# Carrying the minus sign in the queries, so that the masking pass yields minus the row maximum

## The reference

```python
s = jnp.einsum('bqhgd,bjhd->bhgqj', q_c, k_c).astype(F32) * scale
if bias is not None:
    s = s + bias
s = jnp.where(valid, s, -jnp.inf)
if sinks is not None:
    m = jnp.maximum(jnp.max(s, axis=-1, keepdims=True), sk)
    p = jnp.exp(s - m)
    p = p / (jnp.sum(p, axis=-1, keepdims=True) + jnp.exp(sk - m))
else:
    p = jax.nn.softmax(s, axis=-1)
```

## Time and profile before

| | |
|---|---|
| median of 3 runs | 1069.41 us (1069.29 to 1070.34) |
| the profiled execution's own time | 1069.54 us |
| its span, first to last instruction | 1067.7 us |
| busy: PE, PEld, DVE, ACT, POOL | 1058.8, 928.8, 745.3, 627.2, 109.0 us |
| weights and tables read | 190.15 MB, 179 GB/s over the span |
| TensorE clock granted | full in all 40 slices |

### The profile page before, as it was taken

How to read it: one execution, slowest core, us unless ns; L and a number is a source line. 1 busy time by engine, 2 the same in 40 slices (tenths; PEclk the granted TensorE clock), 3 DMA queues, 4 the chain that set the end, 5 groups by cost and what they waited for, 6 DMA issues and landing times.

```text
span 1067.7 us, 16580 instructions
## 1 busy us (share of the span) xinstructions
PE 1058.8 (99%) x6592; PEld 928.8 (87%) x6592; DVE 745.3 (70%) x1130; ACT 627.2 (59%) x1066; POOL 109.0 (10%) x127
## 2 busy tenths in 40 slices
PE   8999999999999999999999999999999999999998
PEld 6988889888888898798888888889889989888887
DVE  6776585898855567768988555957655885766751
ACT  5754465776744567657766444547867644655630
POOL 4020000121100000001111000221000000111100
PEclk9999999999999999999999999999999999999999
DMA  7851356665664665367656656555433546665661
GB/s 267 299 178 60 119 176 224 212 196 173 204 197 162 234 202 173 96 194 244 195 176 208 193 167 226 156 198 178 119 118 119 178 151 202 199 193 170 215 192 39
DMA packets 56956, 192.27 MB, mean 180 GB/s; under 512 B 6832, under 2 KB 9776, under 8 KB 56880
## 3 DMA queue, kind: packets, MB, share of 16 engines
q1 hardware_dynamic: 56880, 191.22, 55.4%
HBM read 190.15 MB, written 1.05 MB: 179 GB/s over the span
## 4 chain that ended last, share of the span: by engine, by line
PE 93%; DVE 3%; POOL 1%; ACT 1%; issue 1%; DMA 0%; DVEq 0%; ACTq 0%; POOLq 0%
PE ps L982 28%; PE ps L1071 19%; PE ps L1063 15%; PE ps L1072 10%; PE ps L1359 5%; PE ps L1233 3%; PE ps L1133 2%; PE ps L1149 2%; PE ps L1170 1%; PE ps L1083 1%; DVE lo L1549 1%; PE ps L1218 1%; PE ps L1417 1%; POOL hr L571 1%; PE ps L1243 1%; ACT hi L626 1%
## 5 line engine op out<-in xcount | busy, mean ns | idle before, releaser
L1549 DVE TENSOR_TENSOR lo<-raw,hi 128x1024 fp32r<-128x1024 f32 (+2 forms) x347 | 430.4, 1262 | 88.1 <-ACT hi L626 85.5
L626 ACT ACTIVATE hi<-raw 128x1024 fp32r<-128x1024 f32 (+2 forms) x347 | 347.6, 1036 | 90.3 <-DMA raw<-in_weights 83.8
L1071 PE MATMUL ps<-y_both,hi 128*128 128x512 f32 x912 | 310.7, 389 | 0.0
L1072 PE MATMUL ps<-y_both,lo 128*128 128x256 f32 x912 | 251.8, 276 | 0.0
L1071 PEld LDWEIGHTS ps<-y_both,hi 128*128 128x128 f32 x912 | 171.2, 188 | 35.6
L1072 PEld LDWEIGHTS ps<-y_both,lo 128*128 128x128 f32 x912 | 171.2, 188 | 0.0
L1063 PE MATMUL ps<-y_both,hi 128*128 128x256 f32 x784 | 138.4, 280 | 0.8 <-DVE lo L1549 0.8
L1063 PEld LDWEIGHTS ps<-y_both,hi 128*128 128x128 f32 x784 | 119.0, 188 | 3.8 <-issue 2.6
L1063 PE MATMUL ps<-y_both,lo 128*128 128x256 f32 x392 | 108.8, 278 | 0.0
L982 PE MATMUL ps<-hi,y_both 128*128 128x512 f32 x352 | 94.1, 382 | 2.7 <-DVE lo L1549 1.4
L982 PE MATMUL ps<-hi,h_hi 128*128 128x512 f32 x294 | 91.0, 391 | 0.0
(11 more groups left out here) (289 smaller groups left out, 1467.5 us busy)
## 6 DMA issues: line engine op xcount, KB each, us to landing
raw<-in_weights SPq DMA_DIRECT2D x331, 512.0 KB, 4.3
gain<-in_gains SPq DMA_DIRECT2D x10, 512.0 KB, 7.7
raw<-in_weights SPq DMA_DIRECT2D x8, 384.0 KB, 7.0
bias<-in_rel SPq DMA_DIRECT2D x16, 128.0 KB, 2.4
raw<-in_weights SPq DMA_DIRECT2D x8, 256.0 KB, 2.5
mem_x<-in_mem SPq DMA_DIRECT2D x2, 512.0 KB, 9.9
h<-in_x SPq DMA_DIRECT2D x2, 256.0 KB, 2.8
h<-in_x SPq DMA_DIRECT2D x1, 512.0 KB, 5.9
```

What stands on the lines that cost most here:

```text
L626: act.activation(hi_at(n)[:, :w], raw_at(n)[:, :w], ACT.Copy).then_inc(hi_done, 1)
L1071: pe.matmul(dst, hi_at(n)[:, at], y_both[:, :, k, :], start=k == 0, stop=False)
L1072: mm = pe.matmul(dst[:, 0:S], lo_at(n)[:, at], y_hi[:, k, :], start=False, stop=k == KD - 1)
L1549: dve.tensor_tensor(lo_at(n)[:, :w], raw_at(n)[:, :w], hi_at(n)[:, :w].bitcast(F32), ALU.subtract).then_inc(lo_done, 1)
```

## The change

In stages a, m, f and x the scores come out negated, because the queries are copied with a negative constant (`scale=-HD ** -0.5`, and the selection matrix `c_pick`, which brings in fox's forget term, has -1 instead of 1). The masks of these stages hold +3e38 instead of -3e38 where a key isn't allowed (`least`). The masking pass takes the minimum, which is minus the row maximum, and writes it into `neg` itself; the negation L1682 and the wait before it are left for stage c alone. ACT's exponentials get a scale of -1 in these stages and wait for `row_max`. Stage a starts its minimum from the negated sink, which a new instruction makes once: `sinks_neg`, 128x8, behind `lb_d`. Stage c keeps its scores, its maximum and its negation.

```diff
-        pick[h, h], pick[64 + h, h] = 1, 1
+        pick[h, h], pick[64 + h, h] = -1, -1
...
-        "c_window": window.astype(f), "c_causal": causal.astype(f), "c_block": block_causal,
+        "c_window": least(window).astype(f), "c_causal": least(causal).astype(f), "c_block": block_causal,
...
+        def sign(stage):
+
+            return 1.0 if stage == "c" else -1.0
...
-                act.wait_ge(maxed, a + 1)
+                if stage == "c":
+                    act.wait_ge(maxed, hh + 1)
+                else:
+                    act.wait_ge(row_max, a + 1)
...
-                    e = act.activation(pr[:, a % 2, c], src, ACT.Exp, bias=neg[:, col, t:t + 1], accum_out=tot[:, col, t:t + 1])
+                    e = act.activation(pr[:, a % 2, c], src, ACT.Exp, scale=sign(stage), bias=neg[:, col, t:t + 1], accum_out=tot[:, col, t:t + 1])
...
-                act.activation(q_t[:, :, b * P:(b + 1) * P], split4(bank(b)), ACT.Copy, scale=HD ** -0.5).then_inc(a_evac, 1)
+                act.activation(q_t[:, :, b * P:(b + 1) * P], split4(bank(b)), ACT.Copy, scale=-HD ** -0.5).then_inc(a_evac, 1)
...
-                    dve.tensor_reduce(top[:, col, :], ps[:, a % 2, :].rearrange("p (t k) -> p t k", t=NT), AX.X, ALU.max).then_inc(row_max, 1)
+                    dve.tensor_reduce(neg[:, col, :], ps[:, a % 2, :].rearrange("p (t k) -> p t k", t=NT), AX.X, ALU.min).then_inc(row_max, 1)
...
-                        init = rows_in[:, hh:hh + 1] if stage == "a" else MASKED
-                        ins = dve.tensor_tensor_reduce(sc[:, a % 2, c], ps[:, a % 2, c], add, 1.0, init, ALU.add, ALU.max,
-                                                       top[:, col, t:t + 1])
+                        if stage == "c":
+                            ins = dve.tensor_tensor_reduce(sc[:, a % 2, c], ps[:, a % 2, c], add, 1.0, MASKED, ALU.add, ALU.max,
+                                                           top[:, col, t:t + 1])
+                        else:
+                            init = sinks_neg[:, hh:hh + 1] if stage == "a" else -MASKED
+                            ins = dve.tensor_tensor_reduce(sc[:, a % 2, c], ps[:, a % 2, c], add, 1.0, init, ALU.add, ALU.min,
+                                                           neg[:, col, t:t + 1])
                     ins.then_inc(row_max, 1)
-                dve.wait_ge(row_max, a + 1)
-                dve.tensor_scalar(neg[:, col, :], top[:, col, :], -1.0, None, ALU.mult).then_inc(maxed, 1)
+                if stage == "c":
+                    dve.wait_ge(row_max, a + 1)
+                    dve.tensor_scalar(neg[:, col, :], top[:, col, :], -1.0, None, ALU.mult).then_inc(maxed, 1)
...
             dve.tensor_tensor(lb_d[:, :], lb_in[:, 0:HB], lb_in[:, HB:2 * HB], ALU.subtract).then_inc(lb_sub, 1)
+            link(dve.tensor_scalar(sinks_neg[:, :], rows_in[:, :], -1.0, None, ALU.mult))
```

More of the change, by code:

```diff
@@ L144, in scores_mask, with least @@
         return np.concatenate([np.where(ok(q, k[:, :P]), 0, MASKED), np.where(ok(q + P, k), 0, MASKED)], 1)
+    def least(mask):
+        return np.where(mask < 0, -MASKED, 0)
     window = scores_mask(lambda a, b: (b // CHUNK <= a // CHUNK) & (b // CHUNK >= a // CHUNK - 2))
@@ L272, in build @@
         top = sb("top", [20, 2])
+        sinks_neg = sb("sinks_neg", [8])
         neg = sb("neg", [20, 2])
@@ L830, in _ @@
                     head_square(t, split4(bank(7)), 4, P)
-            act.wait_ge(maxed, 8)
+            act.wait_ge(row_max, 8)
             act.wait_ge(dve_sink, 1)
@@ L910, in heads_copy @@
                     act.activation(token_half(dst, kh, t), split4(bank(base + b)), ACT.Copy,
-                                   scale=HD ** -0.5 if kh == 0 else 1.0).then_inc(heads_evac, 1)
+                                   scale=-HD ** -0.5 if kh == 0 else 1.0).then_inc(heads_evac, 1)
             def branch_hi(i):
@@ L929, in _ @@
                         act.wait_ge(heads_turned, 8 + t + 1)
-                        act.activation(qc_t[:, :, t * P:(t + 1) * P], split4(bank(4 + t)), ACT.Copy, scale=P ** -0.5).then_inc(heads_evac, 1)
+                        act.activation(qc_t[:, :, t * P:(t + 1) * P], split4(bank(4 + t)), ACT.Copy, scale=-P ** -0.5).then_inc(heads_evac, 1)
                 if k == 1:
@@ L1872, in _ @@
                     even_lo(1, 0, 1)
-                    dve.wait_ge(maxed, 8)
+                    dve.wait_ge(row_max, 8)
                     dve.tensor_tensor(snk, neg[:, 0:8, :], rows_in[:, 0:8].rearrange("p (a b) -> p a b", b=1).to_broadcast([P, 8, 2]),
```

## The result

The changed kernel took 1075.97 us (median of 6 runs, 1074.9 to 1077.04) against 1069.35 us for the kernel before (6 runs, 1068.43 to 1070.34): a ratio of 1.0061, 95% interval 1.0049 to 1.0074. The forecast was 1069.4 with 1070.6 as its upper end, and 0.04 for slower. It is 6.6 us off. The profiled execution took 1075.29 us, its span was 1073.5, TensorE's clock was granted in full.

A forecast was written before the change was run, and what follows sets the result against it. TensorE, busy 99% of the span, was taken as the bound; removed negations, earlier ScalarE and the added costs each counted 0 against the profiled 1069.54 us, giving 1069.4 beside the runs' median of 1069.41; range 1068.3 to 1070.6.

The forecast's parts named there:

- The added `sinks_neg`: Between `lb_d` and even_f's first unit: one negation costing VectorE 0.24 us, up to 2.7 with GpSimd contention, the span 0.
- All four: Rivals: freed time reaching a later wait (0.05), dearer minimum (0.04), `sinks_neg` held longer (0.05), TensorE gaps as hidden waits (0.04).
- `sinks_neg` held longer: Rival, before even_f: held past the 0.2 us left, one low part is late; 1069.4 to 1070.5 us, chance 0.05.
- the prediction's signs of being wrong: TensorE wait at 73-136 or 736-831 us, longer passes, `sinks_neg` over 2.7 us, or span falling by over 1.1 us.
- The removed negations: First and third layers' attention: 28 of 44 go, VectorE busy 5.4 us less, 6.7 us of engine time, path gain 0.
- the row that the prediction took: Third layer's first pair: 0.24 us back per negation, 6.7 in all; the skill's rule would give 3.4.
- ScalarE starts earlier: Stage a's exponentials: 7 x 0.2 us earlier, head 4 1.05 us; third layer's start unmoved; gain 0.
- Minimum for maximum, scale of -1: 48 masking passes, 4 reductions, 56 ScalarE passes: taken as 0; bounds up to +0.94 us a masking pass, ±0.02 for scale.
- The cover, TensorE's own stream: Both edited attention stretches: TensorE waits for no VectorE result following a negation, so the 6.7 us stay off the path.

The follow-up runs named there:

- e1: The kernel before with one unused tile of 32 bytes a partition between `top` and `neg`, no instruction changed: 1075.75 us, ratio 1.0062.
- e2: The changed kernel with the negated sinks kept in free columns of `rec`, so no tile is added: 1069.55 us, ratio 1.0003.
- e12: The changed kernel with `sinks_neg` allocated last in the first layer's list, behind `hw`: 1068.79 us, ratio 1.0001.
- e14: The changed kernel with only the weight units of `down2` starting 32 bytes later in their rings: 1073.92 us, ratio 1.0044.
- e9: The kernel before with 32 unused bytes between the weight rings and all other tiles: 1087.83 us, ratio 1.0176.
- e4: The kernel before with 32 unused bytes between `h_hi` and `h_lo`, and in the tile lists sharing that memory: 1074.13 us, ratio 1.0046.
- e10: The changed kernel with `sinks_neg` last and new `DIST` entries for even_f, even_q, odd_out and merge_out: 1083.4 us, ratio 1.0137.

## Why the prediction was wrong, step by step

- **The added `sinks_neg`** is the step that failed. It was priced as an instruction, and as one it was right: 0.16 us at 26.59, though GpSimd had an operation under way from 25.88 to 26.79, and nothing waits for it. It is also a tile, and the prediction's account of what the change adds never lists the 32 bytes. Their price is the whole loss: `e1` has only them (1075.75), `e2` and `e12` have everything else (1069.55, 1068.79). That nothing waits for the new line was taken for proof that it costs nothing; TensorE was then treated as a bound of fixed length, though its matmuls' rate depends on where their operands lie (233.9 ns in the first down stage and not 227.5).
- **No rival covers it.** All four were waits or dearer instructions. *`sinks_neg` held longer* had the right name for the wrong reason: its price was some 1 us, by GpSimd. The range ended at 1070.6 and could not hold it. Nor did one of the prediction's signs of being wrong appear: they were waits, longer passes, a longer `sinks_neg` and a shorter span, and a TensorE that is busy for longer wasn't among them.
- **The removed negations** were right. 16 are left, and VectorE's busy time is 740.3 us against the 740 expected. `e2` shows their worth on the path: 0, within 1.3 us. In engine time the row that the prediction took is borne out, and not the half of it: in the third layer's first pair the next head's pass came 0.24 us after the accumulator read the earlier trace rows, and now both start together:

```profile
740.07 0.08 DVE L1694 DVE_READ_ACCUMULATOR2_ANT neg<- 128x1 f32 x1
740.07 0.28 DVE L1694 CUSTOM_DVE_ANT_0 sc<-ps,causal 128x128 f32<-128x128 f32 x1
```

- **ScalarE starts earlier**: right in place, a little large in size. Against the earlier trace rows, head 4 of the first layer now reads:

```profile
101.93 0.08 DVE L1694 DVE_READ_ACCUMULATOR2_ANT neg<- 128x1 f32 x1
...
102.05 0.40 ACT L698 ACTIVATE pr<-sc,neg 128x128 f32<-128x128 f32 x1 [0.33 <-DVE neg L1694]
...
107.82 0.49 PE L1161 MATMUL ps<-ident,pr 128*128 128x128 f32 x3
```

The read ends at 102.01 and the exponential starts 0.04 later; before, it started 1.09 after its read. For all eight heads the waits for `neg` fell from the 20.6 us of the earlier trace rows to:

```profile
  DVE neg L1694: 18.6, 8
```

2.0 us less, where 7 x 0.2 + 1.05 = 2.45 were worked out. And it bought nothing, since its last read now ends at 103.04 and TensorE turns these probabilities 4.8 us later.

- **Minimum for maximum, scale of -1**: taken as 0, the lower bounds, and right. The masking passes are at 0.29 and 0.42 us as in the earlier trace rows, the reductions at 0.69:

```profile
L1694 DVE CUSTOM_DVE_ANT_0 sc<-ps,causal 128x256 f32<-128x256 f32 x16 | 6.7, 420 | 0.0
...
L1694 DVE CUSTOM_DVE_ANT_0 sc<-ps,causal 128x128 f32<-128x128 f32 x16 | 4.6, 289 | 17.4 <-PE ps L1148 11.6 <-PE ps L1145 5.8
```

- **The cover, TensorE's own stream**, held in every attention stage. The waits are those of before.

So the forecast was right about the instructions that it priced and wrong about the kernel. With the tile put behind all others it would have held (`e12`, 1068.79, within 0.2% of 1069.4).

## What to carry to other kernels

Where TensorE is busy all the time, a change to the list of tiles is a change to TensorE: before pricing instructions, list what every new or resized tile moves, and by how much relative to the tiles that are read together with it. A small new tile goes last, or the shift is made a multiple that the kernel's own placement repeats at (256 bytes here). Look for a table that places things by unexplained offsets, as `DIST` here; it suggests that distances were tuned. And moving such an offset can have its own price, where a ring's units then wait for other units: here 0.5 to 7 us a place, and none in `e14`.

## What the runs showed of the hardware

- **Two operands' places together set a matmul's rate.** In the down stages the activation tile is the operand that is loaded, and the weight unit streams past it. With both at the same place modulo 256 bytes a 128x512 fp32r matmul took 227 ns from start to start; with the tile moved by 32, 64 or 128 bytes against both rings, 232 to 234 in the mean of the stage. Moved together, or by 256, nothing changed.
- **The same place isn't the best one everywhere.** In the up stages the weights are loaded and `y_both` streams; there a 128x512 matmul took 226.6 ns with the `hi` unit 64 bytes below the tile. The 128x256 matmuls of even_f, also with loaded weights, took 120 ns at the same place modulo 256, 116.7 with the tile 32 bytes up (`e9`), and 113.6 with `hi` 64 bytes above the tile and `lo` 64 below. So these runs give single distances and their rates, and no rule for all stages.
- The Trainium skill (TensorE: Matmul & The Clock Gate, Part 2, Step-by-step) says that TensorE has two independent read ports, so that loading the next tile's weights takes no bandwidth from the running matmul. By that rule no price would be expected from these two reads, wherever they lie. The runs measured 6.6 us, 3% of a down matmul, with no wait on record. They don't show that the two reads collide, so the ports as such aren't disproved, but the place of one operand against the other isn't free. The measurement decides.
- Why is open. A conflict between the load of one operand and the stream of another is a guess that no run tests. In `e4`, where only `h_lo` has moved, even two matmuls in a row on `h_hi` and `hi` stand 231.0 ns apart in the mean of the first two down stages, where 227.2 stood, so the slow pairs aren't only those that read `h_lo`. Nor was a shift by 16 bytes tried, or distances between 128 and 256.
- In `e10` a wait of 7.1 us of TensorE was followed by a clock of 0.50 from 459 to 463 us, so the stall cost more than its own length.
